# Layer 0's output stage: head normalisation on ScalarE, the norm row multiplied into the gates by GpSimd

## The reference, cut to what matters

```python
hs = hf + _rev(hb)                                  # (tokens, 4 heads, 256)
mu = jnp.mean(hs, -1, keepdims=True)
var = jnp.mean(jnp.square(hs - mu), -1, keepdims=True)
hn = (hs - mu) * lax.rsqrt(var + NORM_EPS) * _f32(norm_w).reshape(M_HEADS, M_DV)
y = (jax.nn.sigmoid(_f32(o)) * hn.reshape(Bn, T, hv)).astype(h.dtype) @ w_out
```

## Time and profile before

| | |
|---|---|
| time, median of 3 runs | 4409.89 us (4409.48 to 4415.5) |
| span of the profiled execution, first to last instruction | 4409.3 us |
| mean granted TensorE clock | 0.931 |
| PE, DVE, POOL, ACT busy | 80%, 69%, 57%, 17% of the span |
| scan, from its first load to the output stage | 310.4 to 505.2 us |
| output stage | 505.2 to 634.5 us |

### The profile page before, as it was taken

How to read it: one execution, slowest core, us unless ns; L and a number is a source line. 1 busy time by engine, 2 the same in 40 slices (tenths; PEclk the granted TensorE clock), 3 DMA queues, 4 the chain that set the end, 5 groups by cost and what they waited for, 6 DMA issues and landing times. The chain is left out here.

```text
span 4409.3 us, 41525 instructions
## 1 busy us (share of the span) xinstructions
PE 3529.3 (80%) x11702; PEld 1756.0 (40%) x11702; DVE 3058.1 (69%) x7280; ACT 746.8 (17%) x2088; POOL 2512.6 (57%) x2589
## 2 busy tenths in 40 slices
PE   5987768888888888877977675888888888788876
PEld 3456544334333434422445343333343333333332
DVE  2754578777777777776779467766676766676776
ACT  0011111111111111211024131111111111111221
POOL 0000017767677777776755103777777777777775
PEclk8988889999999999999987787999999999999999
DMA  6731329999999999999987634999999999999998
GB/s 241 252 133 19 110 83 403 405 407 407 398 404 405 399 406 404 401 404 381 371 331 246 209 115 184 408 407 405 405 404 405 401 406 405 401 404 405 402 409 345
DMA packets 453089, 1491.65 MB, mean 338 GB/s; under 512 B 49860, under 2 KB 71236, under 8 KB 452612
## 3 DMA queue, kind: packets, MB, share of 16 engines
q0 software_dynamic: 368640, 1342.34, 77.3%
q1 hardware_dynamic: 80068, 138.34, 9.3%
q10 hardware_dynamic: 4160, 8.39, 0.6%
HBM read 1484.07 MB, written 4.82 MB: 338 GB/s over the span
## 5 line engine op out<-in xcount | busy, mean ns | idle before, releaser
L1629 DVE SCALAR_TENSOR_TENSOR wrk<-wrk,ps 128x1024 f32<-128x1024 f32 x1184 | 1439.9, 1218 | 801.8 <-DMA wrk<-in_peer_u,route_gate 801.2
L1567 POOL DMA_INDIRECT wrk<-in_peer_u,route_gate x1184 | 1124.8, 950 | 729.9 <-issue 458.3
L1431 PE MATMUL ps<-mod,diag 128*128 128x512 f32 x1152 | 568.4, 618 | 153.5 <-DMA mod<-in_peer_v,route_gate 153.2
L1576 POOL DMA_INDIRECT mod<-in_peer_v,route_gate x584 | 567.7, 972 | 178.5 <-issue 158.8
L1431 PE MATMUL ps<-mod,y 128*128 128x512 f32 x1184 | 530.3, 597 | 16.8 <-DMA mod<-in_peer_v,route_gate 16.8
L1431 PE MATMUL ps<-lnw,y 128*128 128x512 f32 x592 | 343.6, 735 | 223.7 <-ACT y L1505 222.7
L1431 PEld LDWEIGHTS ps<-mod,diag 128*128 128x128 f32 x1152 | 197.6, 189 | 516.4 <-DMA mod<-in_peer_v,route_gate 369.2
L1576 POOL DMA_INDIRECT lnw<-in_peer_v,route_gate x292 | 278.1, 952 | 210.9 <-DVE route_gate L1156 121.9
L1431 PE MATMUL ps<-big,diag 128*128 128x512 f32 x576 | 285.5, 618 | 100.5 <-DMA big<-in_peer_v,route_gate 100.5
L1431 PEld LDWEIGHTS ps<-mod,y 128*128 128x128 f32 x1184 | 217.8, 191 | 279.8 <-issue 222.2
L1576 POOL DMA_INDIRECT big<-in_peer_v,route_gate x292 | 276.1, 946 | 89.1 <-issue 73.2
(11 more groups left out here) (517 smaller groups left out, 4291.7 us busy)
## 6 DMA issues: line engine op xcount, KB each, us to landing
wrk<-in_gla_w_in SPq DMA_DIRECT2D x12, 2048.0 KB, 13.1
wrk<-in_peer_u,route_gate POOLq DMA_INDIRECT x1184, 9.3
big<-in_peer_w_q SPq DMA_DIRECT2D x16, 1024.0 KB, 16.7
mod<-modulation_rows SPq DMA_DIRECT2D x22, 512.0 KB, 6.6
lnw<-in_ada_w SPq DMA_DIRECT2D x14, 768.0 KB, 6.0
mod<-in_ada_w SPq DMA_DIRECT2D x40, 256.0 KB, 3.2
qk<-in_ada_w SPq DMA_DIRECT2D x13, 768.0 KB
mod<-in_ada_w SPq DMA_DIRECT2D x13, 768.0 KB, 6.1
```

What stands on the lines that cost most here:

```text
L1431: mm = pe.matmul(m.ps[:, b + h, :], diag[r], ring_v[r % RV][:, h * HALF:(h + 1) * HALF], start=r == 0 and i % 2 == 0, stop=r == on_pe(i) - ...
L1567: pool.indirect_dma_start(ring_u[r % RU], None, u, bass.IndirectOffsetOnAxis(ap=expert_slot(m, slot_at[work[i]])[:, r:r + 1], axis=0)).the ...
L1576: pool.indirect_dma_start(ring_v[r % RV], None, v, bass.IndirectOffsetOnAxis(ap=expert_slot(m, slot_at[work[i]])[:, r:r + 1], axis=0)).the ...
L1629: dve.scalar_tensor_tensor(out=ring_u[r % RU], in0=ring_u[r % RU], scalar=1.0, in1=xm_ps, op0=ALU.mult, op1=ALU.mult, accum_out=act_u[i % ...
```

## The change

In the output stage VectorE no longer computes the four normalised heads and no longer multiplies by the norm row. It computes a shift, -mean * rstd, for the four heads in one small operation, and ScalarE then computes rstd * H + shift for each head with both factors as operands per partition. `head_gate(k)`, the product with the gates, stays on VectorE and follows `head_norm(k)` at once everywhere. ScalarE's four operations stand behind its square root in `sqrt_head(k)`.

The norm row is loaded in the scan, behind the three gate loads, to row 15 of `big`, and GpSimd, after its loop of copies, multiplies it into the gates of the five tiles in place, one operation of 128x1024 per tile. The output stage's load of the norm row is gone.

```diff
@@ mlstm_scan
+        nw = row_of(m.big, 15)
         def _(sp):
             ...
                 sp.dma_start(m_in[d], a["state_mlstm_m"][0, d].partition_broadcast(P)).then_inc(gate_in, 16)
+            sp.dma_start(nw, a["mlstm_norm_w"].partition_broadcast(P)).then_inc(norm_in, 16)
             sp.wait_ge(m_swapped, 4)
         def _(pool):
             ...
             with pool.Fori(1, NT) as i:
                 round_(i)
+            pool.wait_ge(norm_in, 16)
+            for t in range(NT):
+                gate = m.proj[:, t, 4 * HALF:6 * HALF]
+                pool.tensor_tensor(gate, gate, nw, ALU.mult).then_inc(weighed, 1)
@@ mixer_output
+    shift = m.stat[:, 52:56]
         def _(sp):
-            for h in range(n_norm):
-                s = norm_w.shape[0]
-                sp.dma_start(nw[:, h * s:(h + 1) * s], norm_w.partition_broadcast(P)).then_inc(norm_loaded, 16)
             sp.dma_start(W[:, :, 0:HALF], w[:, :, 0:HALF]).then_inc(w_loaded[0], 16)
             def sqrt_head(k):
                 act.wait_ge(head.sem, head.at(k, "eps"))
                 act.activation(var, var, ACT.Sqrt).then_inc(head_act.sem, 1)
+                act.wait_ge(head.sem, head.at(k, "shift"))
+                if k > 0:
+                    act.wait_ge(transposed, k)
+                for h in range(NH):
+                    act.activation(m.y[:, h * DV:(h + 1) * DV], m.H[:, order[k], h * DV:(h + 1) * DV], ACT.Identity,
+                                   scale=var[:, h:h + 1], bias=shift[:, h:h + 1]).then_inc(head_act.sem, 1)
                 dve.reciprocal(var, var).then_inc(head.sem, 1)
                 own("rstd")
-                if k > 0:
-                    dve.wait_ge(transposed, k)
-                for h in range(NH):
-                    dve.tensor_scalar(m.y[:, h * DV:(h + 1) * DV], hh(h), mv[:, h, 0:1], var[:, h:h + 1], ALU.subtract,
-                                      ALU.mult).then_inc(head.sem, 1)
-                own("n3")
-                if k == 0:
-                    dve.wait_ge(norm_loaded, 16 * n_norm)
-                dve.tensor_tensor(m.y[:], m.y[:], nw, ALU.mult).then_inc(head.sem, 1)
-                own("weighed")
-                dve.tensor_tensor(m.y[:], m.y[:], m.proj[:, t, 4 * HALF:6 * HALF], ALU.mult).then_inc(head.sem, 1)
+                dve.scalar_tensor_tensor(out=shift, in0=mv[:, :, 0], scalar=-1.0, in1=var, op0=ALU.mult,
+                                         op1=ALU.mult).then_inc(head.sem, 1)
+
+            def head_gate(k):
+                dve.wait_ge(head_act.sem, head_act.at(k, "n3"))
+                dve.tensor_tensor(m.y[:], m.y[:], m.proj[:, order[k], 4 * HALF:6 * HALF], ALU.mult).then_inc(head.sem, 1)
...
             head_norm(0)
+            head_gate(0)
             head_norm(1)
+            head_gate(1)
             residual(0)
```

More of the change, by code:

```diff
@@ L524, in mlstm_scan @@
             ("dve", "diag"), ("pe", "rows")))
-        pre, cleared, stored, state_in, gate_in, m_swapped = (
-            st.sem(n) for n in ("pre", "cleared", "stored", "state_in", "gate_in", "m_swapped"))
+        pre, cleared, stored, state_in, gate_in, m_swapped, norm_in, weighed = (
+            st.sem(n) for n in ("pre", "cleared", "stored", "state_in", "gate_in", "m_swapped", "norm_in", "weighed"))
+        nw = row_of(m.big, 15)
         block = st.block()
@@ L844, in mixer_output @@
     order = [1, 2, 3, 4, 0]
-    w, norm_w = a["mlstm_w_out"].rearrange("(k p) n -> p k n", p=P), a["mlstm_norm_w"]
+    w = a["mlstm_w_out"].rearrange("(k p) n -> p k n", p=P)
     W = m.wrk[:, 0:KD * D].rearrange("p (k n) -> p k n", k=KD)
-    nw, z = row_of(m.big, 13), row_of(m.big, 15)
+    z = row_of(m.big, 15)
     turned = [m.yT[:], row_of(m.big, 12).rearrange("p (k n) -> p k n", k=KD)]
@@ L852, in mixer_output @@
     var = m.stat[:, 48:52]
-    n_norm = HV // norm_w.shape[0]
+    shift = m.stat[:, 52:56]
     pair_at = lambda b: m.ps[:, b:b + 2, :].rearrange("p b n -> p (b n)")
     with Stage(nc, f"out{layer}") as st:
-        head = Order(st.sem("head"), "b0 b1 b2 b3 a0 a1 a2 a3 eps rstd n0 n1 n2 n3 weighed gated")
+        head = Order(st.sem("head"), "b0 b1 b2 b3 a0 a1 a2 a3 eps rstd shift gated")
         rest = Order(st.sem("rest"), "scaled added " + NORM + " done")
-        head_act, rest_act = Order(st.sem("head_act"), "sqrt"), Order(st.sem("rest_act"), "sqrt")
+        head_act = Order(st.sem("head_act"), "sqrt n0 n1 n2 n3")
+        rest_act = Order(st.sem("rest_act"), "sqrt")
         loaded, transposed, copied, product = (st.sem(n) for n in ("loaded", "transposed", "copied", "product"))
-        passed, norm_loaded = st.sem("passed"), st.sem("norm_loaded")
+        passed = st.sem("passed")
         w_loaded = [st.sem("w_loaded0"), st.sem("w_loaded1")]
@@ L999, in _ @@
             head_norm(2)
+            head_gate(2)
             residual(1)
             head_norm(3)
+            head_gate(3)
             residual(2)
             head_norm(4)
+            head_gate(4)
             front.routes(dve, passed)
```

## The result

The changed kernel takes 4420.46 us (median of 19 runs), the one before 4409.6 us (19 runs on the same chip): a ratio of 1.0025, 95% interval 1.0019 to 1.0032, so 8.4 to 14.1 us slower. The forecast was 4419.9, slower. The profiled span is 4420.8 us against 4409.3, the mean granted clock 0.93 in both.

A forecast was written before the change was run, and what follows sets the result against it. No engine was always busy; in the scan TensorE and VectorE take turns, so either's delay delays the stage. Blocking 10.5 + clock 2.0 - output stage 2.5 = +10.0 us on the 4409.3 span, 4419.9 in run terms; range 4411 to 4424.

The forecast's parts named there:

- The products hold VectorE: Scan, fourth round: five GpSimd products each block a VectorE operation with two SBUF inputs; +10.5 us (5.2 to 13).
- The value between the bounds: Scan: one GpSimd product takes 2.1 us, between a copy's 1.04 and 2.6 for three streams in turn.
- the rival of a product no dearer than a copy: Scan: five products cost 5.2 us, clock loss about 1; +3.7 us in all, 4413.6; chance 0.08.
- The 11.2 us: Scan: estimate for the five products, half of the skill's 4497 ns for 2048 elements, five times.
- The first rival: Scan: GpSimd leaves its loop 6 us late, products find VectorE idle and block nothing; 4407.4 us; chance 0.12.
- TensorE's clock: Scan: longer idle time before L639 makes TensorE's transposes and the product behind them slower; +2.0 us (0 to 2.3).
- the wait before L639: Scan, fourth round: TensorE's idle time ahead of its transposes grows from 4.3 to some 15 us.
- The heads on ScalarE: Output stage, reciprocal to gate: four ACTIVATEs take 1.9 us, saving 0.5 us a tile; 1.0 us for k=2 and k=4.
- table load per tile: Output stage rival: ScalarE's function needs its own table, two loads per tile, +7.7 us, 4427.6; chance 0.03.
- The norm row's load: Output stage, tile k=0: without this load TensorE's second product starts 1.5 us earlier (0.4 to 1.9); in the scan no cost.
- The sum: Whole kernel: 10.5 + 2.0 - 2.5 = +10.0 us, ends +1.9 and +15.1.

The follow-up runs named there:

- experiment 1: The changed kernel with GpSimd's five products waiting until VectorE's last two-SBUF-operand operation of the fourth round has ended; 4412.98 us, ratio 0.9999 to the kernel before.
- experiment 4: The changed kernel with ten GpSimd products in place of five, the norm row multiplied in twice; 4432.45 us, ratio 1.0043 to the kernel before.
- experiment 5: The changed kernel with six GpSimd fills of 128x2048 in place of the five products, norm row left out; 4415.56 us, ratio 1.0015 to the kernel before.
- experiment 7: The changed kernel with products in VectorE's idle stretch and the heads back on VectorE; 4405.46 us, ratio 0.9990 to the kernel before.
- experiment 10: The kernel before with only the heads moved to ScalarE, the norm row still a product on VectorE; 4415.24 us, ratio 1.0005.
- experiment 8: As experiment 1, with VectorE's gates product cut into four operations of one head each; 4406.52 us, ratio 0.9992 to the kernel before.
- experiments 2: The changed kernel without the five products and without the norm row's load; 4410.81 us, ratio 0.9993 to the kernel before.

## Why the prediction was right, point by point

**The products hold VectorE.** Right in place, way and size. They began at 439.00, at once behind the copies, five VectorE operations were held one after the other, and the round lost 10.87 us for 10.5 forecast. Experiments 1 and 4 show that this is the whole loss of the round: without the coincidence nothing, with twice the products 20.8. The value between the bounds (2.1 us, two copies) was near: 2.31 unheld (experiment 1), which also rules out the rival of a product no dearer than a copy. The 11.2 us that the prediction works out from the Trainium skill (GPSIMD Engine Reference, Elementwise — side-by-side cycle accounting), whose figure is for a two-input addition, are near as well: five products unheld took 11.57 us. The first rival's condition was right too, the products free in the idle stretch, but GpSimd was not late.

**TensorE's clock.** Wrong: 2.0 us forecast for the scan, nothing measured there. The step that failed is the reading that after 4.3 us of idle time the transposes (L639) "still run at the upper level". The row shows four of them in 1.12 us, and the prediction set that beside eight in 1.09. Four in 1.12 are the lower level, as the granted clock says: 0.50 while the sixteen transposes ran, before as after. In the first round of experiment 5, at a granted clock of 1.00, four took 0.66. So the round ran its transposes at the lower level already and had nothing left to lose there (experiment 4 has 1.12 after 12.02 us of idle time, again at 0.50). The stretches of these transposes, with the columns of the earlier trace rows, from before, after and experiment 5:

```profile
448.40:452.07 3.67, 3.67 (x16) 3.27 (x16) 0.54 (x1) 1.40 (x3) 0.00 (x0) 0.50 0.00 0
456.59:460.26 3.67, 3.67 (x16) 3.27 (x16) 0.54 (x1) 1.40 (x3) 0.00 (x0) 0.50 0.00 0
334.15:334.75 0.60, 0.60 (x5) 0.60 (x6) 0.54 (x1) 0.00 (x0) 0.00 (x0) 1.00 0.00 0
```

The transposes of experiment 5, and one of two pairs of small matmuls before:

```profile
334.15 0.66 PE L646 MATMUL ps<-cst,wrk 128*128 128x128 f32 x4 [3.98 <-DVE wrk L764]
...
443.73 0.39 PE L635 MATMUL ps<-scr,cst 128*128 128x8 f32 x2 [0.41 <-DVE scr L730]
```

The forecast that the wait before L639 grows to some 15 us failed as well. The two pairs of small matmuls (L635 before, L641 after) stand ahead of the transposes and wait for the same held operations: 8.27 and 2.37 us fell to them, and the wait ahead of the transposes stayed 4.28. These pairs are what did slow down, 0.60 us each at a granted clock of 0.50 for 0.29 and 0.39 at 1.00, and VectorE waited 0.38 us for the second of them instead of 0.17. So the longer wait cost the round about 0.2 us by the clock.

**The heads on ScalarE.** Right in way, too good in size: four ACTIVATEs took 2.07 us, not 1.9, so the step shrank by 0.37 us a tile, not 0.5. What the prediction didn't part is whose gain this is: one norm product less on the path wins 1.26 us (2.71 to 1.45, experiment 7), and ScalarE's heads give 0.89 of it back (1.45 to 2.34; experiment 10 shows the same 0.89 on the other side). As forecast there was no table load per tile, and k=3's transposes came without a wait.

**The norm row's load.** Right: from the stage's first VectorE operation to the start of TensorE's second product it is 20.64 us (513.00 to 533.64) and was 21.98 (505.25 to 527.23), 1.34 won for 1.5 forecast. The load of the second half of the weights sets this start. TensorE itself was ready 2.27 us earlier, because its first product began 0.99 us earlier in the stage and took 8.73 us instead of 10.01, and the difference of 0.93 became a longer wait for the weights, 1.75 us for 0.82.

**The sum.** The output stage won 1.8 us for 2.5 forecast. Beside the two sizes above, TensorE's product behind k=2's transposes took 8.88 us against 8.13, 0.75 more. Here the clock did charge something that the prediction had left out: over the first 3.70 us of that product the mean granted clock was 0.70 before and 0.50 after, and the rest of it ran at the upper level in both. First before, then after:

```profile
553.31:557.01 3.70, 3.70 (x8) 1.61 (x8) 0.00 (x0) 1.01 (x1) 0.00 (x0) 0.70 0.00 0
559.35:563.05 3.70, 3.70 (x6) 1.63 (x6) 0.00 (x0) 1.01 (x1) 0.00 (x0) 0.50 0.00 0
```

Over the kernels this product varies from 7.55 us (experiment 10) to 9.05 (experiment 8); what sets when the clock rises in it no run tells, so whether the 0.75 us are the change's stays open. In place of +10.5 + 2.0 - 2.5 = +10.0 the profile has +10.9 + 0 - 1.8 = +9.1, inside the runs' 8.4 to 14.1. So errors offset each other: a cost that didn't come against a gain that was smaller and a hold that was larger. Without the clock's term the sum would have been +8.0 and the time 4417.9, still within the range; that the forecast lies 0.6 us from the measured median is luck.

## What to carry to other kernels

An idle engine isn't free work: ask what its instructions share with the busy one, and look in the trace for a stretch in which the other does nothing that can be held; one wait that moved five GpSimd products by 8 us took away the 10.9 us that they cost. Split a change into its halves and price each by the step it stands in (here from reciprocal to gate): the half that won (a product less on the path) carried a half that lost (the heads on another engine, 2.07 us for 1.38 and a hand-over more). Before charging a change with a slower clock, find at which level the work runs now, by the granted clock of its own stretch and by times for the same number of instructions. And where an engine's wait is forecast to grow, look for its small instructions in between, since they take the wait on themselves.

## What the runs showed of the hardware that was not expected

- GpSimd's fills hold VectorE nearly as long as its products do (the round 9.1 us longer against 10.9), if VectorE comes to a copy from SBUF to SBUF: a copy of 128x4, 0.16 us by itself, took 9.53 us beside six fills; rewritten with two sources it took 0.15 beside one.
- A two-operand product of 128x1024 on GpSimd takes 2.31 us, 2.2 times a copy (1.04).
- Four ACTIVATEs of 128x256 with scale and bias per partition take 2.07 us, a sixth less than eight of 128x128 with one operand (2.45 in the earlier trace rows).
- Products beside the VectorE operations that they hold don't grow much: 12.50 us for five, 11.57 without.
- With nothing held in it, the scan's fourth round takes from 32.5 us at a mean granted clock of 0.95 (experiments 2, 7) to 34.2 at 0.86 (before, experiments 1, 10), so a round's length from one profile has to be read with its granted clock beside it.
